# Expert gates written by indirect transfers in place of routing matmuls, in a decoder layer on one core

## What is computed

```python
def block(xb):                                          # per token
    q = (xb @ w_q).reshape(TOKEN_BLOCK, 8, 2, 128)
    s = jnp.einsum('thcd,hcnd->thcn', q, sub_keys)
    vals, idx = lax.top_k(s, 16)
    cand = vals[:, :, 0, :, None] + vals[:, :, 1, None, :]
    cand_ids = idx[:, :, 0, :, None] * 128 + idx[:, :, 1, None, :]
    best, pos = lax.top_k(cand.reshape(TOKEN_BLOCK, 8, 256), 16)
    ids = jnp.take_along_axis(cand_ids.reshape(TOKEN_BLOCK, 8, 256), pos, axis=-1)
    g = jax.nn.softmax(best, axis=-1)
    h = jax.nn.gelu(jnp.einsum('td,thkd->thk', xb, u_tab[ids]))
    return jnp.einsum('thk,thkd->td', g * h, v_tab[ids])
```

## Time and profile before

| | |
|---|---|
| median of 3 runs | 3902.0 us (3900.2 to 3908.9) |
| the profiled execution | 3903.9 us |
| its span, first to last instruction | 3902.1 us |
| granted TensorE clock, mean | 0.994 |
| expert stage behind its opening, first block to value stage | 1611 to 2573 us |
| value stage | 2573 to 3652 us |

### The profile page before, as it was taken

The page is one execution under the profiler, slowest core; times in us unless marked ns, Lnnn a source line. Parts: engine busy times, 40 slices in busy tenths (PEclk is TensorE's granted clock), DMA queues, the critical chain, the costliest instruction groups (busy, mean ns, idle before and its releaser), DMA issues.

```text
span 3902.1 us, 57973 instructions
## 1 busy us (share of the span) xinstructions
PE 3808.9 (98%) x20449; PEld 3471.3 (89%) x20449; DVE 2682.2 (69%) x3814; ACT 1403.7 (36%) x1992; POOL 1265.6 (32%) x620
## 2 busy tenths in 40 slices
PE   8999999999998999999999999989999999999999
PEld 6888888878886889999999999989999999999777
DVE  3555555534413899878878878778888888898642
ACT  4433444441114223446546545222222222222442
POOL 4444444434443447422222222212212211222233
PEclk9999999999999999999999999999999999999999
DMA  4222222224433324698998898978877877787332
GB/s 156 95 97 97 102 94 94 94 99 152 148 121 108 108 89 160 232 367 321 361 373 314 340 378 328 404 294 315 306 288 279 318 289 283 285 311 278 119 105 78
DMA packets 210825, 856.40 MB, mean 219 GB/s; under 512 B 17520, under 2 KB 107824, under 8 KB 119216
## 3 DMA queue, kind: packets, MB, share of 16 engines
q1 hardware_dynamic: 137648, 515.62, 36.6%
q0 software_dynamic: 41600, 302.04, 19.2%
q10 hardware_dynamic: 31488, 37.76, 2.7%
HBM read 788.21 MB, written 67.11 MB: 219 GB/s over the span
## 4 chain that ended last, share of the span: by engine, by line
PE 75%; DVE 9%; DMA 7%; DVEq 3%; ACT 3%; issue 2%; ACTq 1%; SPq 0%
PE bank L631 24%; PE bank L633 23%; PE bank L632 23%; DMA raw<-ws 7%; DVE wlo L1611 2%; PE bank L875 2%; DVEq L1625 2%; DVE yacc L1715 2%; ACT whi L1027 1%; DVE sc L1416 1%; PE bank L674 1%; DVEq L1709 1%; PE bank L693 1%; DVE hot L1600 1%; DVE res L1757 1%
## 5 line engine op out<-in xcount | busy, mean ns | idle before, releaser
L1027 ACT ACTIVATE whi<-raw 128x1024 fp32r<-128x1024 f32 x784 | 820.6, 1057 | 2253.9 <-PE bank L633 1429.2
L631 PE MATMUL bank<-ahi,whi 128*128 128x352 f32 (+1 forms) x3968 | 1434.6, 362 | 32.2 <-DVE alo L1365 7.9
L632 PE MATMUL bank<-alo,whi 128*128 128x352 f32 (+1 forms) x3968 | 1413.8, 356 | 0.0
L633 PE MATMUL bank<-ahi,wlo 128*128 128x352 f32 (+1 forms) x3968 | 1413.6, 356 | 0.0
L594 POOL TENSOR_TENSOR wlo<-raw,whi 128x1024 fp32r<-128x1024 f32 x316 | 792.0, 2510 | 1050.3 <-ACT whi L1027 1021.5
L631 PEld LDWEIGHTS bank<-ahi,whi 128*128 128x128 f32 x3968 | 749.8, 189 | 126.7 <-issue 35.9
L633 PEld LDWEIGHTS bank<-ahi,wlo 128*128 128x128 f32 x3968 | 749.4, 189 | 77.3
L632 PEld LDWEIGHTS bank<-alo,whi 128*128 128x128 f32 x3968 | 749.5, 189 | 72.1 <-issue 0.5
L1611 DVE TENSOR_TENSOR wlo<-raw,whi 128x1024 fp32r<-128x1024 f32 x472 | 574.7, 1223 | 190.6 <-ACT whi L1027 188.3
L631 PE MATMUL bank<-xwhi,whi 128*128 128x384 f32 x2048 | 686.7, 335 | 19.3 <-ACT hst L1226 10.3
L633 PE MATMUL bank<-xwhi,wlo 128*128 128x384 f32 x2048 | 685.7, 335 | 0.0
(11 more groups left out here) (218 smaller groups left out, 2809.8 us busy)
## 6 DMA issues: line engine op xcount, KB each, us to landing
raw<-ws SPq DMA_DIRECT2D x394, 1024.0 KB, 4.9
gelu_spill<-hst ACTq DMA_DIRECT2D x128, 192.0 KB, 3.7
route_spill<-gst SPq DMA_DIRECT2D x24, 1024.0 KB, 14.8
hg<-gelu_spill SPq DMA_DIRECT2D x64, 384.0 KB, 6.7
hg<-route_spill SPq DMA_DIRECT2D x64, 384.0 KB, 7.4
gate_spill<-gout ACTq DMA_DIRECT2D x32, 256.0 KB, 2.1
gl<-gate_spill SPq DMA_DIRECT2D x32, 256.0 KB, 2.7
xin<-xT SPq DMA_DIRECT2D x8, 512.0 KB, 8.6
```

The source lines that it names most:

```text
L631: pe.matmul(ps_out, hi, xh, start=first, stop=False)
L632: pe.matmul(ps_out, hi, xl, start=False, stop=False)
L633: return pe.matmul(ps_out, lo, xh, start=False, stop=last)
L1027: act.activation(whi[:, s], raw[:, s // 2, s % 2], ACT.Copy).then_inc(hi_done, 1)
```

## The change

The dense gates are not made on TensorE any more. A DRAM array `expert_spill` holds for every key row, partition and token the gelu (index 0) and the gate (index 1), side by side. Its gate half is zeroed in the first stage from an SBUF tile of zeros, 32 transfers of 768 KB on SP's queue, one after each two units. For the 384 dense columns VectorE computes the offset of each pick in that array (`goff`). For each pick of each 128 tokens (3 x 128 times) it compares the pick's offset with all 128 offsets of its token and sums the gates of the equal ones in one instruction with an accumulator (`sum_gate`, 8 for each 3 blocks: 256 in the first 96 blocks of the tiles, 128 in blocks 112 to 159), and signals each. GpSimd writes each column of 128 sums to the array by an indirect DMA of 128 elements of 4 bytes (`put_gate`). Equal picks write the same sum. The puts stand among the gathers by the lists `EARLY` (256 puts over gathers 0 to 99) and `LATE` (128 over gathers 100 to 149); the first of every sixteen of a column waits until the column's earlier ones have landed. `TILE_DOTS` becomes three of every four blocks. The offsets' and gates' last group has the extra 32 tokens' products hx in its last 32 partitions, which GpSimd copies there at row 74 (`extra_gates`).

Gone with the routing: the one-hots, their scaling, `gst` and its spills, the turned picks, x1's spill and load. `hg` is loaded by one transfer per two rows in place of two, in pieces of 3 KB, from the seventh unit behind the tiles on.

The diff, cut to its core:

```diff
-TILE_DOTS = [j % 2 == 1 or j in (4, 8, 12) if j < 16 else j not in (18, 23, 28) for j in range(32)]
+TILE_DOTS = [j % 4 != 3 for j in range(32)]
...
+EARLY = [(NUP - 60) * j // (2 * NP) for j in range(2 * NP)]
+LATE = [NUP - 60 + 50 * j // NP for j in range(NP)]
...
-    x1_sp = nc.dram_tensor("x1_spill", (P, KD, T), F32).ap()
-    gelu_sp = nc.dram_tensor("gelu_spill", (NK, P, TD), F32).ap()
-    route_sp = nc.dram_tensor("route_spill", (NRT, P, NK * RT), F32).ap()
+    eg_sp = nc.dram_tensor("expert_spill", (NK, P, 2, TD), F32).ap()
+    eg_flat = eg_sp.rearrange("k p c (t o) -> (k p c t) o", o=1)
...
+            sp.wait_ge(const_ok, 1)
+            with sp.Fori(0, NK // 4) as i:
+                for s in range(2):
+                    load_unit(2 * i + s, s)
+                k4 = sp.snap(i * 4)
+                sp.dma_start(eg_sp[bass.ds(k4, 4), :, 1].rearrange("k p t -> p k t"),
+                             zero[:].unsqueeze(1).broadcast_to((P, 4, TD))).then_inc(zero_out, 16)
+            with sp.Fori(NK // 4, (U1 + U1T) // 2) as i:
...
-            def spill_x1(q):
-                sp.wait_ge(ln[1]["lo_ok"], 4 * q + 4)
-                sp.dma_start(x1_sp[:, 4 * q:4 * q + 4], res[:, 4 * q:4 * q + 4]).then_inc(x1_out, 16)
...
-            def tile_loads(t):
-                expert_loads(2 * PRE + 16 * t, 5)
-                tt = sp.snap(t)
-                sp.wait_ge(g_evac, t * GT + (2 + GT))
-                for q in range(6):
-                    n = NK * RT // 4
-                    if q < 4:
-                        sp.dma_start(route_sp[tt, :, q * n:(q + 1) * n], gst[:, q * n:(q + 1) * n]
-                                     ).then_inc(tile_out, 16)
-                    load_unit(16 * t + (B5 // 2 + 2 * PRE + 10 + q), q % 2)
...
             def load_hg(k, s):
                 k2 = sp.snap(k * 2)
-                sp.dma_start(hg[:, s, 0].rearrange("p (c t) -> p c t", c=2),
-                             gelu_sp[bass.ds(k2, 2)].rearrange("c p t -> p c t")).then_inc(hg_in[s], 16)
-                kk = sp.snap(k * 2 * RT)
-                sp.dma_start(hg[:, s, 1].rearrange("p (a x) -> p a x", a=NRT),
-                             route_sp[:, :, bass.ds(kk, 2 * RT)].rearrange("a p x -> p a x")
+                sp.dma_start(hg[:, s], eg_sp[bass.ds(k2, 2)].rearrange("k p c t -> p k c t")
                              ).then_inc(hg_in[s], 16)
-            expert_loads(0, PRE)
-            with sp.Fori(0, NRT) as t:
-                tile_loads(t)
+            expert_loads(0, U4 // 2 + POST)
             for k in range(2 * (64 - POST)):
                 load_unit(B5 // 2 + 2 * POST + k, k % 2)
-                if k == 1:
-                    sp.wait_ge(tile_out, 64 * NRT)
-                    sp.wait_ge(g_full, TD // 4)
+                if k == 2:
+                    sp.dma_start(pin[:], pT).then_inc(p_in, 16)
+                if k == 6:
+                    for a in range(TD // P):
+                        sp.wait_ge(put[a], 16 * NP)
                     for s in range(2):
                         sp.wait_ge(gelu_out[s], 16 * 4)
-                    sp.dma_start(pin[:], pT).then_inc(p_in, 16)
-                if k in (2, 4):
-                    load_hg(k // 2 - 1, k // 2 - 1)
-                if k in (3, 5, 7, 11):
-                    q = (3, 5, 7, 11).index(k)
-                    sp.dma_start(res[:, 4 * q:4 * q + 4], x1_sp[:, 4 * q:4 * q + 4]).then_inc(x1_in, 16)
+                    for s in range(2):
+                        load_hg(s, s)
                 if k in (9, 10):
...
+            def put_gate(a, n):
+                if n == 0:
+                    pool.wait_ge(offs_ok, 1)
+                    pool.wait_ge(zero_out, 16 * NK // 4)
+                pool.wait_ge(sum_ok, (n // TOPK * 2 + a) * TOPK + n % TOPK + 1 if a < 2 else 2 * NP + n + 1)
+                if n % TOPK == 0 and n:
+                    pool.wait_ge(put[a], 16 * n)
+                nc.gpsimd.indirect_dma_start(
+                    eg_flat, bass.IndirectOffsetOnAxis(ap=goff[:, a, n:n + 1], axis=0),
+                    gval[:, a, n:n + 1], None).then_inc(put[a], 16)
+            def extra_gates():
+                pool.wait_ge(hx_w, 1)
+                for j in range(NJ):
+                    pool.dma_start(gone[P - NX:P, TU // P, j * NXP:(j + 1) * NXP],
+                                   hx[j * NX:(j + 1) * NX]).then_inc(xw_in, 16)
+            def put_gates(n):
+                for j, at_row in enumerate(EARLY):
+                    if at_row == n:
+                        put_gate(j // TOPK % 2, j // (2 * TOPK) * TOPK + j % TOPK)
+                if n == NTG * 3 + 2:
+                    extra_gates()
+                for j, at_row in enumerate(LATE):
+                    if at_row == n:
+                        put_gate(TU // P, j)
+            def gather_rows(first, n_rows, table, rows, gates=False):
                 for n in range(n_rows):
                     s = n % RING
                     nc.gpsimd.indirect_dma_start(
                         rows[:, s], None, table,
                         bass.IndirectOffsetOnAxis(ap=idxs[:, s, 0:1], axis=0)).then_inc(rows_in[s], 16)
+                    if gates:
+                        put_gates(n)
             lo_parts(0, DVE_LO)
             spread_picks()
-            gather_rows(0, NUP, u_tab, urows)
+            gather_rows(0, NUP, u_tab, urows, gates=True)
             gather_rows(NUP, NP, v_tab, vrows)
...
-            def route(g, s):
-                pe.wait_ge(hot_scaled, g + 1)
-                pe.wait_ge(g_evac, g + 1)
-                for k in range(4):
-                    mm = pe.matmul(ps_g[s][:, k * P:(k + 1) * P], hot1[:, s, k], hot2w[:, s, k],
-                                   start=True, stop=True)
-                mm.then_inc(g_full, 1)
-            def expert_step(i, g=None):
+            def expert_step(i):
                 for s in range(2):
                     pe.wait_ge(evac5, i * 2 + (s + 1))
                     for half in range(2):
                         one_block(i * 4 + (B5 + 2 * s + half), 2 * s + half, s, half, n=TU)
-                        if g is not None:
-                            route(g + (2 * s + half), half)
...
-            def scale_hots(g, s):
-                act.wait_ge(hot_ok, g + 1)
-                for k in range(4):
-                    sc2 = act.activation(hot2w[:, s, k], hot2[:, s, k], ACT.Copy,
-                                         scale=gT[:, bass.ds(4 * g + k, 1)])
-                sc2.then_inc(hot_scaled, 1)
-            def take_group(t, g, s):
-                act.wait_ge(g_full, GT * t + g + 1)
-                act.activation(gst[:].rearrange("p (k t) -> p t k", t=RT)[:, bass.ds(4 * g, 4), :],
-                               ps_g[s][:].rearrange("p (t k) -> p t k", t=4), ACT.Copy).then_inc(g_evac, 1)
...
-                        act.dma_start(gelu_sp[i * 2 + u], hst[:, u]).then_inc(gelu_out[u], 16)
+                        act.dma_start(eg_sp[i * 2 + u, :, 0], hst[:, u]).then_inc(gelu_out[u], 16)
...
-            dve.wait_ge(picks_full, 1)
-            dve.tensor_copy(gT[:], ps_s[0][:, 0:TD])
-            dve.tensor_copy(i1T[:], ps_s[1][:, 0:TD])
-            dve.tensor_copy(i2T[:], ps_x[:, 0:TD])
+            dense = slice(0, TD // P)
+            dve.scalar_tensor_tensor(gflat[:].rearrange("p a n -> p (a n)"),
+                                     i2n[:, dense].rearrange("p a h k -> p (a h k)"), float(NK),
+                                     i1n[:, dense].rearrange("p a h k -> p (a h k)"), ALU.mult, ALU.add)
+            dve.tensor_copy(gone[:].rearrange("p a n -> p (a n)"),
+                            gn[:, dense].rearrange("p a h k -> p (a h k)"))
             dve.drain()
-            def one_hots(t, g):
-                s, g = g % 2, GT * t + g
-                tok = bass.ds(4 * g, 4)
-                for dst, src in ((hot1, i1T), (hot2, i2T)):
-                    oh = dve.tensor_tensor(dst[:, s], src[:, tok].unsqueeze(2).broadcast_to((P, 4, P)),
-                                           iota[:].unsqueeze(1).broadcast_to((P, 4, P)), ALU.is_equal)
-                oh.then_inc(hot_ok, 1)
-            def hots_free(t, g):
-                dve.wait_ge(g_full, GT * t + (g - 1))
+            for a in range(TD // P):
+                dve.tensor_scalar(gflat[:, a], gflat[:, a], 2.0 * TD, gcol[:, a:a + 1], ALU.mult, ALU.add)
+            dve.drain()
+            dve.tensor_copy(goff[:].rearrange("p a n -> p (a n)"), gflat[:].rearrange("p a n -> p (a n)"))
+            dve.drain().then_inc(offs_ok, 1)
...
+            def sum_gate(j):
+                if j < 2 * NP:
+                    a, n = j // TOPK % 2, j // (2 * TOPK) * TOPK + j % TOPK
+                else:
+                    a, n = TU // P, j - 2 * NP
+                if j == 2 * NP:
+                    dve.wait_ge(xw_in, 16 * NJ)
+                dve.scalar_tensor_tensor(same[:], gflat[:, a], gflat[:, a, n:n + 1], gone[:, a], ALU.is_equal,
```

(71 more changed lines are left out.)

92 lines of the change are left out of this document (15 added, 77 removed).

## The result

The changed kernel takes **3975.8 us** (median of 4 runs, 3968.2 to 3977.5) where the kernel before takes 3901.5 beside it: ratio 1.0183 [1.0164 to 1.0201], slower by 74 us. The prediction was 3970. The profiled execution took 3976.0, its span is 3974.2.

The account below looks back on a forecast made before the run. GpSimd's indirect DMAs, held up by VectorE, were to bound the expert stage: 899 + 28 + 20 + 84 + 2 - 4 = 1029 us where 961.5 were, +68, so 3970 us; range 3850 to 4075.

Parts of the forecast that it names:

- The gain: Expert stage without routing: at most 132 us less, 86 of routes and 46 of stalls.
- The sums: 384 sums on VectorE at 0.43 us each, making its own pace 4.21 us a block.
- The puts held up: Blocks with sums: GpSimd's indirect DMAs wait for VectorE instructions with two SBUF inputs; 4.73 us a block over 144 blocks.
- Rival 1: GpSimd is not held up by the sums; VectorE bounds blocks with sums, TensorE the others: 3848 us, chance 0.22.
- The blocks without sums: 50 expert-stage blocks without sums, with about 9 indirect DMAs issued in TensorE's 15.36 us: 4.36 us a block.
- The start: Stage start: gathers behind puts that wait for sums lay bare waits before dots 1, 2 and 4; 28 us.
- The late waits: Last 128 puts, one column: every sixteenth waits for the one before to land; 20 us, bounds 0 and 42.
- The last 22 blocks: The expert stage's other 22 blocks, at TensorE's 3.84 us each: 84 us.
- The zeros: 32 issues of 768 KB on SP's queue in the first stage: no cost, up to 32 x 2 us if loads came late.
- The value stage: As before, starting about 2640, with 2 us of wait at its start where TensorE had waited 10.3.
- Rival 2: Four-byte writes are dear for the DMA engines: at 100 ns each 5.12 us a block, 4064 us; chance 0.12.
- Rival 3: Everything cancels: holds cost half, 4.38 us a block throughout, no late-wait loss, within 0.2% of before; chance 0.04.

Follow-up runs that it names:

- no_both: Changed kernel without the puts and the sums (the output lacks the gates); 3768.1 us, 0.9661 of the kernel before.
- no_puts: Changed kernel without the 384 puts, sums and dots kept (the output lacks the gates); 3826.3 us, 0.9809 of the kernel before.
- no_sums: Changed kernel without the 384 sums; the puts write each pick's own gate, the signal stays in VectorE's order; 3975.4 us.
- psum_all: Changed kernel with all dots, the extra ones too, reading their second input from PSUM instead of SBUF, except rows 32 to 35; 3877.7 us.
- two_arrays: Changed kernel with the odd heads of the extra group (64 of 384 puts) written to a second array that nobody reads; 3949.5 us.
- plain_writes: Changed kernel with the puts replaced by 384 plain writes of 128 x 4 bytes to a spare array from ScalarE's queue; 3828.2 us.
- full: psum_all with the puts' heads interleaved, sums spread evenly (2 per block over 192 blocks) and the first put behind gather 4; 3836.2 us.
- psum_dots: Changed kernel with the second input of 128 dots in PSUM instead of SBUF, the 32 extra dots still reading SBUF; 3932.9 us.

## Why the prediction was right

The sign and the mechanism held: 74 us slower where 68 were predicted, because GpSimd's indirect DMAs are held up by VectorE and the row gathers stand behind the puts. The size is closer than its parts. The terms in order:

- **The gain.** At most 132 us in the stage, 86 of routes and 46 of stalls. no_both measured 122 there, and 8 more in the value stage.
- **The sums.** 0.43 us each was too low: they stand 0.48 apart. By that VectorE's own pace would be (4.56 + 7.71 + 10.67 x 0.48)/4 = 4.35 in place of 4.21; no_puts ran at 4.27. It would have cost some 9 us (144 x 0.06) if VectorE had been the bound; it was not (no_sums).
- **The puts held up, 4.73 us a block.** Blocks 7 to 95 took 4.53 to 4.68, a little less, and the hold was shown by taking it away (psum_all, -98 us). TensorE was busy for 0.89 and 0.84 of the two stretches from 1700 on where 0.80 to 0.88 were forecast, and a put took 1.47 us where some 1.5 were. The rule of the Trainium skill that a VectorE instruction with two SBUF inputs contends with a GpSimd instruction that reads SBUF (SBUF — State Buffer, Who interferes with whom) agrees with the trace: an indirect DMA has its offsets in SBUF, and a put that started in a low part took 1.80 us against 0.97. The Trainium skill also infers, in the same section, that a tensor_tensor does not hold up descriptor generation. I had read the earlier trace rows as against this, and that was wrong: the rows are all of indirect DMAs, and the plain ones of no_puts passed a low part and a dot unheld, as inferred. Whether it is the reading of the offsets that is held, no run separates. Rival 1, which took the inference to cover the puts, fell.
- **The blocks without sums, 4.36 us.** Too low. Blocks 96 to 111 took 4.60 and blocks 160 to 191 took 4.91, and even without the late waits 4.57 (two_arrays); that is some 10 us over the 48 blocks beside the late waits. I had taken it that more room on VectorE lets more puts through.
- **The start, 28 us.** The waits before dots 1, 2 and 4 come to 17.9 us, and the edit that removes them gives 18.5. Place and cause were right by the trace: the put ahead of gather 1 waited 4.98 us for its sum, the next such puts 8.60 and 5.19. The size was a third too large.
- **The late waits, 20 of 0 to 42.** They are worth 26.
- **The last 22 blocks at 3.84.** This is the term that was furthest off. From block 192 to the value stage it took 114 us where 95 were counted (two blocks at 4.36, 22 at 3.84, 2 of wait). no_puts needed some 12 us less for the same 24 blocks: the last put started at 2569.6, and the last gathers stood behind it (blocks 192 to 203 took 5.09 us each). The wait at the value stage was 6.25 us and not 2.
- **The zeros, nothing.** The tiles' first low part starts at 1606.5, 3.4 us earlier than before.
- **The value stage, as before.** It was 8 us shorter. There `hg` comes in one transfer per two rows of 3 KB pieces in place of two; ScalarE's waits for raw fell from 355 to 90 us in it. What of this brought the 8 us was not tried.

Added up along the stage, the first 96 blocks took 18 us less than the sum has for them (464 against 482), the next 96 took 9 more (465 against 456), and the rest 19 more; with a start 2 us later than counted, the stage came out at +80 and not +68, and the value stage gave 8 back. That such errors cancel is luck; the mechanism is not. Rival 2 (four-byte writes dear) is refuted by plain_writes as far as regular addresses go, and by a DMA share of 0.85 at 303 GB/s where it wanted a full one. Rival 3 had the blocks at 4.38, where they took 4.5 to 4.9.

The granted clock is separated only in part. It was 0.982 in the mean in place of 0.994, and 0.90 to 0.96 in the stretches in which TensorE waited; full had 0.992. For the same 19672 matmuls TensorE was busy 3767.8 us in the changed kernel and 3725.8 in no_puts, so up to 42 of the puts' 150 us came by way of the clock, behind the waits. The 43 us of psum_dots did not: its TensorE was busy 3774.1 us at a mean clock of 0.981. Of the further 55 us of psum_all (3738.0 us busy), up to 36 may be clock.

## What to carry to other kernels

Count the instructions of a queue, not only their bytes: 384 indirect DMAs moved 0.2 MB, cost the data path nothing that could be measured, and took 150 us: each is some 1.3 us of GpSimd at best, 1.8 with the holds, and the row gathers stood behind them. If GpSimd issues indirect DMAs beside VectorE, look where VectorE's second input lies: moving one operand of the long instruction to idle PSUM banks left its duration alone and took 98 us off. Test a schedule only after the bound is removed: the same order and spread lost 39 us before that edit and gained 23 after it.

## What the hardware showed that was not expected

- A dot of 128x2048 takes 2.29 us whether its second input lies in SBUF or in PSUM, but only the first kind holds up an indirect DMA (2.06 against 0.97 us in the rows above). Plain DMAs of GpSimd are not held by it (four in 2.07 us beside it, in 2.08 alone).
- While GpSimd was the bound, VectorE's order decided how fast it went: the same 384 sums spread evenly cost 61 us more than in bursts, with 0.26 us more per indirect DMA that began in a dot.
- 384 plain writes of 128 x 4 bytes, 3 KB apart, made no difference that could be measured (3828.2 against 3826.3 us).
